# A float32 decoder trunk: one fetch of the input weights makes the projections of two or three token tiles

## The reference, cut to what matters

```python
proj = h @ w_in                              # 1024 -> 1824 columns
qa, ka, va, u, cq, ckv, kr = jnp.split(proj, cuts, axis=-1)
ya = dilated_attention(norm(qa), norm(ka), va, biases)      # 6 heads, sliding windows
yb = s5_mixer(u, *s5_params)                                # diagonal state space, a scan over tokens
yc = mla_attention(q(cq), k(ckv, kr), v(ckv))               # 6 heads, latent attention
x = x + g1 * (concat(norm(ya), norm(yb), norm(yc)) @ w_out)

q = h2 @ wq                                  # h2: second modulated norm of x
top_s, top_i = top_k(q . subkeys, 16)        # two sides of 8 heads
best, experts, gates = top 16 of the 16 x 16 sums, softmax   # 128 experts per token
act = gelu(einsum('td,tkd->tk', h2, u_tab[experts]))
x = x + g2 * einsum('tk,tkd->td', gates * act, v_tab[experts])
```

## Time and profile before

| | |
|---|---|
| median of 3 runs | 3233.72 us (3227.81 to 3236.72) |
| profiled execution, span | 3239.0 us (the profile gives no time beside the span) |
| PE, DVE, ACT, POOL busy | 2362.4, 2336.7, 1515.7, 1143.2 us (73%, 72%, 47%, 35%) |
| moved by DMA | 1310.00 MB, mean 404 GB/s |
| by POOL's gathers | 1073.81 MB, 80.4% of the 16 engines' span |
| by SyncE's transfers | 232.65 MB, 18.1% |
| chain that ended last | DMA 41%, PE 27%, DVE 14%, ACT 7% |

### The profile page before, as it was taken

One profiled execution on the slowest core, in us unless ns is written; L12 is line 12 of the kernel. 1 busy time (PEld: TensorE's weight loads), 2 busy tenths in 40 slices (PEclk: granted clock), 3 DMA queues, 4 the chain that ended last, 5 costly groups with the idle time before them and its releaser, 6 DMA issues.

```text
span 3239.0 us, 45251 instructions
## 1 busy us (share of the span) xinstructions
PE 2362.4 (73%) x15268; PEld 1189.2 (37%) x15268; DVE 2336.7 (72%) x6331; ACT 1515.7 (47%) x4895; POOL 1143.2 (35%) x1029
## 2 busy tenths in 40 slices
PE   7786678677785777757687678867687677875555
PEld 5372334333452434514243333524344243441111
DVE  6478856878668778677767776677766877688554
ACT  2225454455544455454544545445553545545443
POOL 0004333333333333333443333334333334434442
PEclk7787979878987889978898887978888799888777
DMA  9859999999999999999999999999999999999997
GB/s 365 359 204 420 413 420 409 419 416 420 415 415 415 408 418 398 415 419 418 419 412 418 409 417 420 415 410 411 418 409 418 408 419 420 393 417 414 422 421 323
DMA packets 204830, 1310.00 MB, mean 404 GB/s; under 512 B 26333, under 2 KB 41869, under 8 KB 52278
## 3 DMA queue, kind: packets, MB, share of 16 engines
q0 software_dynamic: 147456, 1073.81, 80.4%
q1 hardware_dynamic: 56422, 232.65, 18.1%
q10 hardware_dynamic: 720, 0.66, 0.1%
HBM read 1302.15 MB, written 7.16 MB: 404 GB/s over the span
## 4 chain that ended last, share of the span: by engine, by line
DMA 41%; PE 27%; DVE 14%; ACT 7%; issue 4%; POOL 3%; SPq 0%; ACTq 0%; DVEq 0%; POOLq 0%
DMA ringbuf<-in_p_uv,IDX 37%; PE PS L1053 14%; DVE ringbuf L1953 8%; PE PS L973 3%; PE PS L1012 3%; POOL ringbuf L674 3%; PE PS L816 2%; ACT v_th L1415 2%; DMA WB<-in_p_wi 2%; ACT v_w L1424 2%; ACT DIAG L1431 2%; PE PS L747 1%; DMA WB<-in_p_ada 1%; ACT v_sq L1412 1%; PE PS L893 1%
## 5 line engine op out<-in xcount | busy, mean ns | idle before, releaser
L674 POOL DMA_INDIRECT ringbuf<-in_p_uv,IDX x1024 | 1142.8, 1116 | 2067.6 <-PE PS L1053 1670.9
L1053 PE MATMUL PS<-ringbuf,DIAG 64*64 64x512 f32 x8192 | 1271.4, 747 | 740.6 <-ACT DIAG L1431 722.0
L1953 DVE SCALAR_TENSOR_TENSOR ringbuf<-ringbuf,H 128x1024 f32<-128x1024 f32 x1024 | 1240.4, 1222 | 592.0 <-DMA ringbuf<-in_p_uv,IDX 587.3
L1053 PEld LDWEIGHTS PS<-ringbuf,DIAG 64*64 64x64 f32 x8192 | 308.2, 155 | 1415.5 <-ACT DIAG L1431 964.2
L1412 ACT ACTIVATE v_sq<-v_y 128x2 f32<-128x2 f32 x512 | 104.4, 204 | 1337.7 <-DVE ringbuf L1953 1337.7
L1415 ACT ACTIVATE v_th<-v_sq,v_y 128x1 f32<-128x1 f32 x1024 | 340.5, 379 | 17.1
L1424 ACT ACTIVATE v_w<-v_th,v_g 128x1 f32<-128x1 f32 x800 | 266.1, 379 | 37.3
L1012 PEld LDWEIGHTS PS<-HT,WB 128*128 128x128 f32 x1888 | 232.0, 204 | 72.5 <-issue 56.9
L1012 PE MATMUL PS<-HT,WB 128*128 128x128 f32 x1888 | 243.1, 290 | 7.0 <-DMA WB<-in_p_wq 6.1
L1431 ACT ACTIVATE DIAG<-fold,v_w 128x64 f32<-128x64 f32 x800 | 234.7, 340 | 13.0
L816 PE MATMUL PS<-WB,HT 128*128 128x256 f32 (+2 forms) x816 | 182.3, 380 | 39.4 <-DMA WB<-in_p_wi 39.4
(11 more groups left out here) (327 smaller groups left out, 2531.4 us busy)
## 6 DMA issues: line engine op xcount, KB each, us to landing
WB<-in_p_wq SPq DMA_DIRECT2D x59, 1024.0 KB, 12.1
WB<-in_p_wi SPq DMA_DIRECT2D x37, 1024.0 KB, 9.4
ringbuf<-in_p_ahead SPq DMA_DIRECT2D x20, 1024.0 KB, 8.0
WB<-in_p_ada SPq DMA_DIRECT2D x16, 1024.0 KB, 15.2
ringbuf<-in_p_uv,IDX POOLq DMA_INDIRECT x1024, 12.6
WF<-in_p_ada SPq DMA_DIRECT2D x12, 1024.0 KB, 12.0
WB<-in_p_wi SPq DMA_DIRECT2D x14, 768.0 KB, 9.3
WB<-in_p_wo SPq DMA_DIRECT2D x8, 1024.0 KB, 14.2
```

The lines of the kernel that those rows point to most:

```text
L674: pool.indirect_dma_start(out=ring[n % RING], out_offset=None, in_=table, in_offset=bass.IndirectOffsetOnAxis(ap=IDX[:, k % 2, s:s + 1], a ...
L1053: mm = pe.matmul(PS[half:half + HALF, 2 * c + r, :], DIAG[r * HALF:(r + 1) * HALF, (n + q) % DIAGS, :], row[r * HALF:(r + 1) * HALF, D + c ...
L1953: dve.scalar_tensor_tensor(row, row, GELU_T, H2[:, k % 2, :], ALU.mult, ALU.mult, accum_out=Y[:, b, q:q + 1]).then_inc(dotted, 1)
```

## The change

Tiles 1, 4 and 6 (*hosts*) and their *guests* share a fetch: tile 1 has guests 2 and 3, tile 4 has 5, tile 6 has 7. When a chunk of input weights has come for a host, PE uses it for the host's product and then for its guests'. Tiles 2, 3, 5 and 7 fetch none.

```diff
@@ -43,8 +43,12 @@
 BATCH = 2
 STEEP = 4
 STAIR = STEEP * TOPK + (TOPK - STEEP) * STEEP
-LARGEST = 3
-GROUPS_OF = [(1, 1, 2, 3, 1)] + [(2, 2, 3, 1)] * (TILES - 1)
+LARGEST = 4
+GUESTS = {1: (2, 3), 4: (5,), 6: (7,)}
+HOSTED = [g for j in sorted(GUESTS) for g in GUESTS[j]]
+HOST_OF = {g: j for j in GUESTS for g in GUESTS[j]}
+OWN = [j for j in range(TILES) if j not in HOSTED]
+GROUPS_OF = [(1, 1, 2, 3, 1)] + [(1, 2, 4, 1) if j in GUESTS else (2, 2, 3, 1) for j in range(1, TILES)]
 LOT = LARGEST * TOPK
 PAIRS = SLOTS // 2
 RING = 8
@@ -180,6 +184,10 @@
 LATE_AT = (1, 3, 5, 8, 10, 12)
 LATE_GATE = 9
 START, PHASE = clocks()
+FRONT = [START[j] - 8 if len(GUESTS.get(j, ())) == 2 else START[j] for j in range(TILES)]
+SHIFT = 4
+APACE = 0.86
+STAGES = 4
 CROWDED = 14
 
 
@@ -190,7 +198,50 @@
 
 def at(j, step):
 
-    return START[j] + step + (2 if step >= 4 else 0)
+    return START[j] + step + (2 if step >= 4 else 0) + (SHIFT if step >= 12 and j in GUESTS else 0)
+
+
+def products(j):
+
+    return [(i, n) for i in range(8) for n in (j, *GUESTS.get(j, ()))]
+
+
+def product_at(j, p):
+    i, n = products(j)[p]
+    if j not in GUESTS:
+        return START[j] + (4 if i == 0 else 6 + i)
+    if p == 0:
+        return FRONT[j] + 4
+    return FRONT[j] + 6.8 + APACE * (p - 1) + (0.9 * max(0, GUESTS[j].index(n)) if i == 0 else 0.9 * (len(GUESTS[j]) - 1))
+
+
+def spilled():
+
+    return [(i, g) for j in sorted(GUESTS) for i in range(6) for g in GUESTS[j]]
+
+
+def evacuated():
+
+    return {c: n + 1 for n, c in enumerate(c for j in OWN for c in products(j) if c != (0, j))}
+
+
+def unfinished():
+
+    return {c: n + 1 for n, c in enumerate(c for j in OWN for c in products(j) if c[1] != (j, *GUESTS.get(j, ()))[-1])}
+
+
+def fold_at(k):
+
+    return 3 if k in GUESTS else 0
+
+
+def norm_clock(j):
+
+    if j in HOSTED or j >= TILES:
+        return []
+    if j not in GUESTS:
+        return [(at(j, 1), j)]
+    return [(FRONT[j] + 1, j)] + [(FRONT[j] + 3.4 + 3 * n, g) for n, g in enumerate(GUESTS[j])]
 
...
-        wi = [("wi", j, i) for i in range(8)]
+        wi = [("wi", j, i) for i in range(8)] if j in OWN else []
         if j == 0:
```

```diff
+
+            def load_guest(j, g):
+                if g == GUESTS[j][0]:
+                    if j >= 2:
+                        sp.wait_ge(dotted, SLOTS * (j - 1))
+                else:
+                    sp.wait_ge(n1_h, g)
+                if g < T:
+                    src = a["x"][0, g * P:(g + 1) * P, :]
+                else:
+                    sp.wait_ge(xf_out, 16 * (g - T + 1))
+                    src = xend[g - T]
+                sp.dma_start(guest_x(j), src).then_inc(xg_in, 16)
+
+            def store_early(i, g):
+                e = kept_out.index((i, g))
+                lo = 0 if i == 0 else WIDE + (768, 1024, 0, 256, 512)[i - 1]
+                w = PIECES[i][1]
+                sp.wait_ge(wi_ev, copied[(i, g)])
+                sp.dma_start(fronts[HOSTED.index(g)][:, lo:lo + w], ST[:, e % STAGES, 0:w]).then_inc(early_out[e % STAGES], 16)
+
+            def load_early(j):
+                n = HOSTED.index(j)
+                sp.wait_ge(s_mm, PH * j)
+                if j >= 2:
+                    sp.wait_ge(folded, j - 1)
+                for e in range(len(kept_out) - STAGES, len(kept_out)):
+                    done = [o for o, (_, g) in enumerate(kept_out) if g <= j and o % STAGES == e % STAGES]
+                    sp.wait_ge(early_out[e % STAGES], 16 * len(done))
+                sp.dma_start(UT[:, :, :].rearrange("p h n -> p (h n)"), fronts[n][:, 0:WIDE]).then_inc(ut_in, 16)
+                sp.dma_start(PRJ[:, :], fronts[n][:, WIDE:]).then_inc(prj_in, 16)
 
...
-                        sp.wait_ge(ahead_mm, len(AHEAD))
-                    if c == ("wi", j, 1):
+                        for g in GUESTS.get(j, ())[1:]:
+                            load_guest(j, g)
+                    if c in (("wi", j, 1), ("uk", j, 0)) and j >= 2 and (c[0] == "wi") == (j in OWN):
                         load_x(j)
+                        if j in GUESTS:
+                            load_guest(j, GUESTS[j][0])
                         if j == T:
                             keep(1)
-                        if j >= 2:
-                            store_f(j - 2)
+                        store_f(j - 2)
+                        if j in HOSTED:
+                            load_early(j)
+                    if c[0] == "wi" and c[2] >= 2:
+                        for g in GUESTS.get(j, ()):
+                            store_early(c[2] - 2, g)
                     if c == ("uk", 1, 0):
                         ahead_stored(sp)
                         for i in range(2):
```

PE's products (the numbers of matmuls are the same as before, in another order), and ACT's copies:

```diff
-                    if i == 5:
-                        pe.wait_ge(rotated, 2 * j + 1)
-                        drive(1)
+                if j in OWN:
+                    for p, (i, m) in enumerate(products(j)):
+                        if i == 0:
+                            continue
+                        yield product_at(j, p)
+                        n, w = number[("wi", j, i)], PIECES[i][1]
+                        pe.wait_ge(w_in[slot[n]], turn[n])
+                        if p >= 2:
+                            input_copied(pe, j, p - 2)
+                        for k in range(KD):
+                            last = pe.matmul(PS[:, 4 + p % 2, 0:w], input_of(m, k), weights(n)[:, k * w:(k + 1) * w],
+                                             start=(k == 0), stop=(k == KD - 1))
+                        last.then_inc(in_mm if (i, m) in partly else w_done, 1)
+                        if (i, m) == (3 if guests else 5, j):
+                            pe.wait_ge(rotated, 2 * j + 1)
+                            drive(1)
+                else:
+                    yield at(j, 9)
+                    pe.wait_ge(rotated, 2 * j + 1)
...
                         act.activation(SQ[:, 0:768], PRJ[:, 0:768], ACT.Square).then_inc(sq_q, 1)
+
+                if j in OWN:
+                    for step in range(2 if j == 0 else 0, 3):
+                        yield from owe(FRONT[j] + step)
+                        yield FRONT[j] + step
+                        head(j, step)
+                    if guests:
+                        for step in range(2):
+                            yield from owe(FRONT[j] + 2.4 + step)
+                            yield FRONT[j] + 2.4 + step
+                            head(guests[0], step)
+                    for p, (i, n) in enumerate(products(j)):
+                        if i == 0 and n in guests:
...
+                        if i >= 6:
+                            dst = VS[:, tt, (i - 6) * 192:(i - 5) * 192]
+                        elif n != j:
+                            e = kept_out.index((i, n))
+                            if e >= STAGES:
+                                act.wait_ge(early_out[e % STAGES], 16 * (e // STAGES))
+                            dst = ST[:, e % STAGES, 0:w]
+                        else:
+                            lo = (768, 1024, 0, 256, 512)[i - 1]
+                            dst = PRJ[:, lo:lo + w]
+                        act.activation(dst, made, ACT.Copy).then_inc(wi_ev, 1)
+                        for c, lo in ((2, 768), (5, 0)):
+                            if products(j)[p - 1] == (c, j):
+                                act.wait_ge(wi_ev, copied[(c, j)])
+                                squares(lo)
+                    yield from owe(math.inf)
+                else:
+                    for step, lo in ((8, 768), (11, 0)):
+                        yield from owe(at(j, step))
+                        yield at(j, step)
+                        act.wait_ge(prj_in, 16 * (HOSTED.index(j) + 1))
+                        squares(lo)
+                    yield from owe(math.inf)
                 more = beside(j)
```

More of the change, by code:

```diff
@@ L215, in gate_clock, with gates_after @@
     return [lot[-len(LOT_COSTS)] for lot in route_clock(j)]
+def gates_after(j):
+    clock = list(zip(gate_clock(j), itertools.count()))
+    return clock[-1:] if j + 1 == TILES else [c for c in clock[:-1] if c[0] > FRONT[j + 1]] + clock[-1:]
 def ada_rows(j):
```

234 lines of the change are left out of this document (139 added, 95 removed).

## The result

The changed kernel takes 3267.6 us in the median (3258.5 to 3274.6), the kernel before 3231.8 beside it: ratio 1.0109, 95% interval 1.0091 to 1.0128. It is slower by 36 us, where the prediction had 3209 and a range of 3186 to 3230. The profiled execution takes 3270.3 us at a span of 3268.5.

The account below looks back on a forecast made before the run. The prediction took DMA transfers to set the pace, with about 6.1 us of slack in the ring. It summed 52 - 3 - 7 - 3 - 14 = 25 us gained: span 3214, median 3209 us, range 3186 to 3230.

Parts of the forecast that it names:

- Removed transfers: Input weights no longer fetched for tiles 2, 3, 5, 7, net 21.9 MB less: 52 us gained, bounds 45 and 55.
- The start: Tile 1's x, square and norm now precede pair 0, delaying the first dot product: 3 us lost, bounds 0 and 10.
- Tile 1's front: Tile 1's work up to its attention: 24 products make PE's work outlast the DMA's; 7 us lost, bounds 0 and 17.
- What I cost at nothing: Next phase's indices, SyncE's stores behind ACT's copies, and UT and PRJ loads: all in time, no loss.
- Tiles 4 and 6: Their fronts, 16 products in about 15 pairs, PE slightly over DMA: 3 us lost for both, bounds 0 and 14.
- The fronts of tiles 2, 5 and 7: Eight pairs each where DVE's work, with a lot's end moved in, exceeds the reduced DMA time: 14 us lost, bounds 5 and 27.
- Tile 3: Its front has no such lot; DVE's 42.4 us fit into 43.9 us of transfers: nothing lost.
- The slower one: Rival, chance 0.08: guests' products on PE wait for ACT's copies, 1.5 us unhidden for each of 56; median 3266 us.
- what was to show it: Slower rival's sign: DMA shares under 0.9 in fronts of 1, 4 and 6, with PE waiting for ACT's copies.

Follow-up runs that it names:

- e1: Changed kernel with, in tile 1's front, ScalarE's three late PRJ squares and TensorE's drive(1) both put behind product (5, tile 1); 3245.4 us, ratio 1.0034.
- e7: Kernel before, without guests, with TensorE's drive(1) behind product 1 instead of 5, four pairs earlier in every tile; 3323.6 us, ratio 1.0297.
- e8: e1 with the guests' products of pieces 1 to 7 taking 2 of 8 contraction steps; 3245.3 us, ratio 1.0048.
- e6: e1 with the 16 scans of each hosted tile covering 16 of their 128 columns; 3235.7 us, ratio 1.0014.
- e14: e1 with steps from the twelfth two pairs later in tiles 2, 5, 7, fold moved, and ScalarE's PRJ copy behind RS in hosted tiles; 3238.9 us, 1.0010.
- e11: Kernel before with TensorE's drive(1) behind product 3 instead of 5, two pairs earlier; 3236.8 us, ratio 1.0024.
- e5: e1 with steps 4 to 11 of hosted tiles (TensorE's drives, VectorE's first rotations, scan, products) put three pairs earlier; 3264.0 us, ratio 1.0116.

## Why the prediction was wrong

*Removed transfers, 52 us*: right, 50 by the page's share of SyncE's queue, 51 by the packets' time. The prediction sets its 421 GB/s against the Trainium skill's 358. In the section that it names (DMA: Bandwidth & Descriptors, section "Bandwidth") that is the share of a core when both cores of a memory domain stream, and a single core is given 425 for a transfer of 16 MB, so the 421 of this one core agree with it. The 2 us of "Anatomy of one DMA" are given there for GpSimd's path and as time until the landing is confirmed; that the queue's time fell by what the bytes are worth fits that.

*The start, 3 us*: no run can tell it from nothing. I had x asked for at 236.1 us and the first dot product at 248.0; SyncE asked at 231.56, and it came at 242.2, where the kernel before has 243.6. From one kernel to the next of those run here it moves between 234.1 and 246.5. The first eight pairs then took 43.7 us instead of 40.3, with 0.9 more of idle time.

*Tile 1's front, 7 us (0 to 17)*: this step failed, by the wait that it had wrong and not by the load. It lost 32 us in 16 pairs, and its 36 us of idle time in place of 7 are more than half of the whole miss. It did not decide by itself that nothing is gained: without its two waits e1 is still 0.34% slower than before. I divided TensorE's busy time by the time of the transfers and never asked, of the steps that the diff moved, what they wait for. drive(1) went from behind 17 pairs to behind 13, and VectorE's rotation stayed at 17; the squares went ahead of the lot over whose buffer they are written. Both could be read beforehand, in the condition `(3 if guests else 5, j)` of the diff and in the wait for `idx_done` that the squares have in both kernels. e1 shows 22 us for the two, e7 the mechanism by itself. Even the 7 had a wrong basis: e8 takes 30 us of TensorE's work away and gains nothing. The 10 us left in phase 0 were inside my bounds by luck: not for TensorE's load, and their cause is open.

*What I cost at nothing*: "ACT has room" was true of the average (47% busy) and beside the point; ScalarE stood for 23 us with room to spare. The indices I looked at only for gathers, not for whoever writes over the lot's buffers. SyncE's stores and the loads of UT and PRJ were hidden, as forecast: no engine's list of waits has UT or PRJ, and TensorE's wait for input weights (WB) before the products of chunks 1 to 7 fell from 39.4 to 1.0 us.

*Tiles 4 and 6, 3 us (0 to 14)*: 7 of idle time. TensorE was nearly as full as forecast; the transfers kept their pace, a share of 1.01.

*The fronts of tiles 2, 5 and 7, 14 us (5 to 27)*: the mechanism was right and the size too small. The eight pairs were forecast at 47 to 50 us; they took 50.1 to 50.3, with VectorE busy 48.5 of them. But the transfers had 38.6 us of work there (0.77 of 50.1), not 43.3, since SyncE issues no load at all in these pairs of tile 2, and no slack came off: 11 us idle each, 33 in all, over the bound of 27. That VectorE is the bound there e6 and e14 show. *Tile 3, nothing*: 44.2 us against 43.9 forecast, 2.7 idle in its phase.

By the table, 36 us of idle time stand in place of 7 in phase 0, 33 in place of 14 in phases 1, 4 and 6, 7 in place of 3 in phases 3 and 5, and 3 in place of none in phase 2: 55 more than forecast. The gathers' packets took 7 us longer (2611.4 against 2604.7, not explained), and the start gave 4 where I took 3 off, which cancel. A gain of 25 forecast and a loss of 30 measured in the profiled executions are 55 apart.

*The rivals.* The slower one had the right number, 3266, from the wrong place: product after product waiting for ScalarE. In the 127.5 us TensorE's waits before guest products do not appear among the fourteen largest; two waits for VectorE did the most of it. It was the right kind of thing, a wait that drains the ring, and had 0.08; that its number came true is luck. So is half of what was to show it: the shares in tile 1's front are under 0.9, as written, but not with TensorE waiting for ScalarE's copies.

*A reading.* The "32 dot products" of the first paragraph are 16 with their 16 reads of the accumulator, as the earlier trace rows count them; the 8 pairs, and all that follows, are right.

## What to carry to other kernels

Where engines run ahead of one another over a ring, count for each step that moves how many turns its engine has done there and how many the work that it waits for needs; the ring covers only a small difference, and less than its depth (here 4 pairs; a gap of two cost 3 us in one front and nothing that shows in six (e11), of three 4 to 9 (e5, where other steps moved too), of four 11 to 16 (e7)), and busy shares say nothing of it. Check the engine that was not moved too: a step does not come earlier because its time in the table does, if other work stands ahead of it in the queue. A busy TensorE is no bound until taking work away from it shortens something.
